# Where the state-space parameters are loaded, when GpSimd starts a round, and five small changes

## The reference, cut to what matters

```python
xn = rmsnorm(x, norm_g);  proj = xn @ w_in          # ten slices: u_a z_a q k v z_b g_a g_b
y_a, h_last = s5_scan(u_a, h0, A, log_dt, B, C, D)  # 64 groups of 16 channels, 64 complex states
y_a = gelu(y_a);  y_a = y_a * sigmoid(y_a @ glu_w + glu_b) * silu(z_a)
o = stick_breaking_attention(q, k_all, v_all, bias) * silu(z_b)   # 8 heads of 128
merged = sigmoid(g_a) * (y_a @ w_branch_a) + sigmoid(g_b) * (o @ w_branch_b)
y = rmsnorm(x + merged @ w_out, norm_f)
```

## Time and profile before

| | |
|---|---|
| median of 3 runs | 3057.72 us (3056.51 to 3058.63) |
| the profiled execution: its time / its span | 3058.2 us / 3056.1 us |
| PE busy | 2973.0 us (97%) |
| DVE / ACT / POOL busy | 1354.0 (44%) / 1017.8 (33%) / 478.9 (16%) |
| mean granted TensorE clock | 0.994 |
| DMA, mean over the span | 108 GB/s |
| one round | about 266 us |

### The profile page before, as it was taken

One profiled execution on the slowest core, in us unless ns is written; L12 is line 12 of the kernel. 1 busy time (PEld: TensorE's weight loads), 2 busy tenths in 40 slices (PEclk: granted clock), 3 DMA queues, 4 the chain that ended last, 5 costly groups with the idle time before them and its releaser, 6 DMA issues.

```text
span 3056.1 us, 48771 instructions
## 1 busy us (share of the span) xinstructions
PE 2973.0 (97%) x19132; PEld 2908.1 (95%) x19132; DVE 1354.0 (44%) x2556; ACT 1017.8 (33%) x1210; POOL 478.9 (16%) x1126
## 2 busy tenths in 40 slices
PE   5999999999999999999999999999999999999997
PEld 5999999999999999999999999999999999999997
DVE  6624443462444346244434524443465444422266
ACT  6135215413521541352154136115422321211142
POOL 6400330050033015003301400330013000000000
PEclk8999999999999999999999999999999999999999
DMA  6231333233223323323322331332438754342283
GB/s 180 79 105 56 87 83 100 72 80 104 63 83 83 98 72 82 105 67 81 84 91 72 86 105 63 91 81 87 138 122 293 247 188 156 94 129 69 79 245 111
DMA packets 425730, 329.29 MB, mean 108 GB/s; under 512 B 64738, under 2 KB 387890, under 8 KB 423474
## 3 DMA queue, kind: packets, MB, share of 16 engines
q1 hardware_dynamic: 425522, 326.34, 35.6%
HBM read 235.72 MB, written 73.73 MB: 101 GB/s over the span
## 4 chain that ended last, share of the span: by engine, by line
PE 78%; POOL 6%; DVE 6%; issue 3%; SPq 3%; ACT 2%; DMA 2%; POOLq 0%; DVEq 0%; ACTq 0%
PE acc L1794 70%; PE side L1759 3%; PE side L1935 2%; DMA work<-work 1%; SPq L501 1%; POOL work L1253 1%; POOL work L1256 1%; POOL work L1254 1%; PE side L1930 1%; POOL work L1259 1%; POOL work L1255 1%; ACT w_high L901 1%; POOL work L1260 1%; DVE work L1528 1%; DMA work<-t_state_seeds 0%
## 5 line engine op out<-in xcount | busy, mean ns | idle before, releaser
L1794 PE MATMUL acc<-x_high,w_high 128*128 128x344 f32 (+2 forms) x5440 | 1221.2, 327 | 16.1 <-ACT w_high L901 3.6
L1794 PE MATMUL acc<-x_low,w_high 128*128 128x344 f32 (+2 forms) x5440 | 1181.0, 320 | 0.0
L1794 PE MATMUL acc<-x_high,w_low 128*128 128x344 f32 (+2 forms) x5440 | 1177.0, 319 | 0.0
L1794 PEld LDWEIGHTS acc<-x_high,w_high 128*128 128x128 f32 x5440 | 908.6, 188 | 37.5 <-issue 17.6
L1794 PEld LDWEIGHTS acc<-x_low,w_high 128*128 128x128 f32 x5440 | 921.8, 189 | 0.0
L1794 PEld LDWEIGHTS acc<-x_high,w_low 128*128 128x128 f32 x5440 | 913.0, 188 | 0.0
L1373 DVE TENSOR_TENSOR w_low<-w_raw,w_high 128x1024 fp32r<-128x1024 f32 x233 | 294.6, 1264 | 612.2 <-ACT w_high L901 609.2
L901 ACT CAST w_high<-w_raw 128x1024 fp32r<-128x1024 f32 x232 | 242.3, 1044 | 940.7 <-PE acc L1794 863.9
L1244 POOL COPY work<-s_tables 128x28 f32 x16 | 3.3, 208 | 1521.1 <-DMA work<-t_state_seeds 1487.7
L1521 DVE TENSOR_TENSOR work<-work,side 128x128 f32<-128x128 f32 x64 | 18.4, 288 | 317.4 <-PE side L1935 317.4
L1759 PE MATMUL side<-work 128*128 128x128 f32 (+5 forms) x704 | 129.4, 312 | 10.0 <-POOL work L1263 10.0
(11 more groups left out here) (305 smaller groups left out, 2435.3 us busy)
## 6 DMA issues: line engine op xcount, KB each, us to landing
w_raw<-in_w_in SPq DMA_DIRECT2D x160, 512.0 KB, 3.9
w_raw<-in_w_out SPq DMA_DIRECT2D x48, 512.0 KB, 3.9
work<-t_sig_ga SPq DMA_DIRECT2D x24, 516.0 KB, 4.2
out<-work SPq DMA_DIRECT2D x18, 512.0 KB
t_qk<-stage SPq DMA_DIRECT2D x16, 516.0 KB, 5.1
work<-t_qk SPq DMA_DIRECT2D x16, 516.0 KB, 4.5
t_sig_gb<-stage SPq DMA_DIRECT2D x16, 516.0 KB, 4.4
t_sig_ga<-stage SPq DMA_DIRECT2D x16, 516.0 KB, 4.3
```

Source lines behind the costliest of these rows:

```text
L1794: ins = mm(acc[s][:, a, 0:n], w[b][:, kk, :], x[:, kx, c0:c0 + n], start=start, stop=stop)
```

## The change

1. `s5_params` of half 0 becomes `load_s5`. For round 0 it is called ahead of the first round; for the others at chunk 19 of the round in front, behind waits for the last scan of attention (`arg_ready`), for `ha_ready` and for `kv_sent`. The small buffers `pw`, `turn` and `u_new` move to the end of the work buffer.
2. GpSimd's half 0 waits for `oz_ready` of the last attention block (step 79) as well as for the parameters.
3. KM of half 0 moves from step 12 to step 11.
4. In the prologue VectorE scales tiles 6 and 7 (between `x_low` of tiles 2 to 5) in place of ScalarE, and ScalarE writes `S_neg` and `S_in` in place of VectorE.
5. The product of keys and query (8 tokens) moves from GpSimd to VectorE, ahead of the sum.
6. TensorE's first column of branch a waits for the seventh GLU gate, its second for the eighth; before, the first waited for the eighth.
7. `new_sums` is cut into pieces at points 21, 22 and 23; the square root and the scaling of the new rows follow at 24 and 25 instead of 22 and 23.

```diff
@@ build
+    c.at = WORK - (12 * HG + 6 * HG + NEW)
     pw = c.take(12 * HG)
@@ sync
+        def load_s5(g0):
+            Bv = [x[0, bass.ds(g0, HG)].rearrange("g n c -> n g c") for x in (B_re, B_im)]
+            sp.dma_start(BcX[0:64], Bv[0]).then_inc(s5_in, 16)
...
+            for f in range(2):
+                sp.dma_start(h12[:, f], t_h[f][...]).then_inc(s5_in, 16)
+        load_s5(0)
@@ s5_params(hf), hf == 0
-                    sp.wait_ge(oz_sent, i * 16 + PRIMED)
-                    sp.wait_ge(kv_sent, i * 80 + PRIMED)
+                    sp.wait_ge(arg_ready, i * 8 + 8 + PRIMED)
+                    sp.wait_ge(ha_ready, i * 2 + 2)
+                    sp.wait_ge(kv_sent, i * 80 + 80 + PRIMED)
+                    load_s5(i * (2 * HG) + 2 * HG)
@@ sync phase_a, after ahead(cn) and send
                 if cn == 0:
+                    sp.wait_ge(oz_sent, i * 16 + PRIMED)
+                    s5_seeds(0)
+                if cn == CHUNKS - 1 and not last:
                     s5_params(0)
-                    s5_seeds(0)
@@ step table
-    ..., KM, ... = ..., (12, 27), ...
+    ..., KM, ... = ..., (11, 27), ...
@@ scalar, prologue
-        act.wait_ge(den_ready, 3)
-        for n in (6, 7):
-            nc.scalar.mul(x_block(n), x_block(n), nrstd[:, NEW + n:NEW + n + 1]).then_inc(x_scaled_a, 1)
+        act.wait_ge(par_mm, 3)
+        nc.scalar.mul(S_neg[0:64]..., acc[0][0:64, 0, :]..., -1.0)
+        nc.scalar.copy(S_in..., acc[0][:, 0, :]...).then_inc(s_seed_ready, 1)
@@ gpsimd
-                if hf == 1:
+                if hf == 0:
+                    pool.wait_ge(oz_ready, 8 * i + PRIMED)
+                else:
                     pool.wait_ge(y_mm, 2 * i + 1)
...
-        for b in range(NEW):
-            pool.wait_ge(pg_k[b % 2], 32 * (b // 2 + 1))
-            pool.wait_ge(q_in[b % 2], 16 * (b // 2 + 1))
-            nc.gpsimd.tensor_tensor(kb, kb, qbc[b % 2]..., ALU.mult).then_inc(kq_done, 1)
@@ vector, prologue
-        for n in range(2, KT):
+        for n in range(2):
+            x_low(2 + 2 * n)
+            x_low(3 + 2 * n)
+            scale(6 + n)
+        for n in range(6, KT):
             x_low(n)
@@ vector, branch a
-                dve.wait_ge(kq_done, n + 1)
+                dve.wait_ge(pg_k[n % 2], 32 * (n // 2 + 1))
+                dve.wait_ge(q_in[n % 2], 16 * (n // 2 + 1))
+                ch(V.tensor_tensor(kb, kb, qbc[n % 2]..., ALU.mult))
@@ vector, last output part
                 if at == 21:
-                    new_sums()
+                    new_added()
+                if at == 22:
+                    new_sums(range(2))
                 if at == 23:
+                    new_sums(range(2, 4))
+                    new_variance()
+                if at == 25:
@@ tensor, branch a
-        pe.wait_ge(glu_n, FT)
         for n in range(KT):
-            if n >= 2:
+            if n < 2:
+                pe.wait_ge(glu_n, FT - 1 + n)
+            else:
                 pe.wait_ge(br_a, n - 1)
```

More of the change, by code:

```diff
@@ L308, in build @@
     pg_in, pg_k, pg_v, q_in = sem("pages_in"), [sem("page_k0"), sem("page_k1")], [sem("page_v0"), sem("page_v1")], [sem("q_in0"), sem("q_in1")]
-    kq_done, zs_part, zs_tr, sarg_ready, sl_ready, sw_ready, sw_tr, swt_ready, spv_mm, ozs_ready = [sem(s) for s in
-        ("kq_done", "zs_part", "zs_tr", "sarg_ready", "slog_ready", "sw_ready", "sw_tr", "swt_ready",
+    zs_part, zs_tr, sarg_ready, sl_ready, sw_ready, sw_tr, swt_ready, spv_mm, ozs_ready = [sem(s) for s in
+        ("zs_part", "zs_tr", "sarg_ready", "slog_ready", "sw_ready", "sw_tr", "swt_ready",
          "spv_mm", "ozs_ready")]
@@ L453, in s5_params @@
                 if hf == 0:
-                    sp.wait_ge(oz_sent, i * 16 + PRIMED)
-                    sp.wait_ge(kv_sent, i * 80 + PRIMED)
+                    sp.wait_ge(arg_ready, i * 8 + 8 + PRIMED)
+                    sp.wait_ge(ha_ready, i * 2 + 2)
+                    sp.wait_ge(kv_sent, i * 80 + 80 + PRIMED)
+                    load_s5(i * (2 * HG) + 2 * HG)
                 else:
                     sp.wait_ge(ha_ready, i * 2 + 1)
-                g0 = i * (2 * HG) + hf * HG
-                Bv = [x[0, bass.ds(g0, HG)].rearrange("g n c -> n g c") for x in (B_re, B_im)]
-                sp.dma_start(BcX[0:64], Bv[0]).then_inc(s5_in, 16)
-                sp.dma_start(BcX[64:128], Bv[1]).then_inc(s5_in, 16)
-                sp.dma_start(BmX[0:64], Bv[1]).then_inc(s5_in, 16)
-                sp.dma_start(BmX[64:128], Bv[0]).then_inc(s5_in, 16)
-                for f in range(2):
-                    sp.dma_start(h12[:, f], t_h[f][:, bass.ds(g0 * NEW, HG * NEW)].rearrange("p (g b) -> p g b", g=HG)).then_inc(s5_in, 16)
+                    load_s5(i * (2 * HG) + HG)
             def s5_seeds(hf):
@@ L866, in _ @@
         nc.scalar.mul(C_neg.rearrange("p (a n) -> p a n", a=2), side[:, :, :], -1.0).then_inc(seed_ready, 1)
+        act.wait_ge(par_mm, 3)
+        nc.scalar.mul(S_neg[0:64].rearrange("p (g b) -> p g b", b=NEW), acc[0][0:64, 0, :].rearrange("p (b g) -> p g b", b=NEW), -1.0)
+        nc.scalar.copy(S_in.rearrange("p (g b) -> p g b", b=NEW), acc[0][:, 0, :].rearrange("p (b g) -> p g b", b=NEW)).then_inc(s_seed_ready, 1)
         for n in range(KT + 3, KT + 5):
@@ L1116, in _ @@
                     nc.scalar.activation(hstd1[:, :], hvar1[:, :], ACT.Sqrt).then_inc(std_ready, 1)
-                if at == 22:
+                if at == 24:
                     act.wait_ge(var_ready, 6)
@@ L1682, in weigh, with new_added @@
             c2(V.tensor_tensor(hs, hs, nf[:, f, :].unsqueeze(1).broadcast_to([P, B2, P]), ALU.mult))
-        def new_sums():
+        def new_added():
             dve.wait_ge(osm_tr, 1)
@@ L1689, in new_sums @@
                                    acc[s][0:NEW, 1:3, :].rearrange("p a (f n) -> p (a f) n", f=4), ALU.add))
-            for q in range(4):
+        def new_sums(quarters):
+            for q in quarters:
                 sq = stage[q % 2][0:NEW, 768:768 + 2 * P].rearrange("p (f n) -> p f n", f=2)
@@ L1695, in new_sums, with new_variance @@
                     c2(V.tensor_reduce(newsum[0:NEW, 2 * q + e:2 * q + e + 1], sq, axis=AX.XY, op=ALU.add))
+        def new_variance():
             n8 = newvar[0:NEW, :]
@@ L1781, in x_transposes @@
             for b in range(4):
-                if k == 0 and 4 * half + b < 6:
+                if k == 0:
                     pe.wait_ge(x_scaled_v, 4 * half + b + 1)
-                elif k == 0:
-                    pe.wait_ge(x_scaled_a, b - 1)
                 last = tr(x_bank(n)[:, b * P:(b + 1) * P], x_block(4 * half + b)[:, k, :], ident[:, :])
```

17 lines of the change are left out of this document (9 added, 8 removed).

## The result

| | before | changed |
|---|---|---|
| median of 3 runs | 3057.72 us | 3031.97 us (3030.60 to 3033.47) |
| profiled execution: its time / its span | 3058.2 / 3056.1 us | 3033.47 / 3031.7 us |
| ratio of times, 95% interval | | 0.9907 (0.9894 to 0.9920) |

The quotient of the two medians is 0.9916 (25.8 us) and lies inside the interval; the ratio in the table is not this quotient and stands for 28 us. The forecast for a median was 3033 with a range of 3027 to 3045. Between the two profiled executions the sum of the terms was 24.6; their spans differ by 24.4. Eight terms that come out within 0.2 in sum need not be right one by one, so the trace is read term by term first.

A forecast was written before the change was run, and what follows sets the result against it. TensorE, busy for 97% of the span, was taken as the bound, with at most 83 us to win. 4.85 + 9.1 + 3.3 + 1.7 + 1.7 + 1.5 + 0.5 + 1.9 = 24.6 off 3058.2 gave 3033.6, median 3033, range 3027 to 3045.

The forecast's parts named there:

- KM one step up (4.85 + 9.1): Rounds: KM at step 11 removes TensorE's waits at YM of half 0 (4.85 us) and KM of half 1 (9.1).
- left-over of 0.13 per round: KM of half 1: wait for GpSimd expected to remain, 0.13 us per round, making 10.0 us into 9.1.
- the prediction's sign against itself: Forecast wrong if GpSimd's half 1 still begins at a landing, or a branch a column waits above 2 us.
- The early start gives TensorE nothing by itself: Rounds: GpSimd's half 0 starts 8.9 us earlier, worth nothing alone to TensorE, but lets KM move a step up.
- Prologue and round 0 (3.3): Start of the kernel to YM of round 0: the chain comes 3.3 us sooner, bounds 1 and 6.
- the 0.7 of the seeds: Round 0: part of GpSimd's first start coming about 2.0 us earlier, 0.7 of it from the state seeds.
- The clock (1.7 + 1.7): Low clock behind standstills: 1.7 us back in round 7, 1.7 in round 0 (bounds 0 and 3.4).
- GLU (1.5): GLU stage: the key product off GpSimd ends TensorE's 1.5 us wait for a low part, bounds 0 and 1.5.
- Branch a (+0.5): Branch a: the earlier door gives 1.2 us, a late low part takes 0.7, leaving 0.5; bounds -2.8 and 1.2.
- the price of the slid queue: Branch a: VectorE's queue slides about 2.3 us once, at column 0, so TensorE stands about 0.7 at column 6.
- Rival C: Branch a: the key product enters the loop feeding it, 27.7 us in standstills and clock, 3062 us in all; chance 0.03.
- Last part (1.9): Last part: cutting point 21's adding into three removes TensorE's 1.9 us standstill, bounds 0.5 and 2.5.

The follow-up runs named there:

- early_only: The kernel before with half 0's parameters loaded early and GpSimd's half 0 started early, KM still at step 12: 3055.86 us, ratio 0.9991.
- km11_only: The kernel before with only KM of half 0 moved from step 12 to step 11: 3039.71 us, ratio 0.9934 to the kernel before.
- no_prologue: The changed kernel with ScalarE scaling tiles 6 and 7 again and VectorE writing the state seeds: 3031.04 us, ratio 0.9906 to the kernel before.
- keys_door: The kernel before with only the key products on VectorE and branch a's door opened by the seventh gate: 3056.42 us, ratio 0.9988.
- keys_twice: The changed kernel with the product of keys and query made twice for each token: 3036.12 us, ratio 0.9922 to the kernel before.
- km12: The changed kernel with KM of half 0 back at step 12: 3051.73 us, ratio 0.9969 to the kernel before.

## Why the prediction was right, step by step

The main mechanism was right, and so were its places. That the sum came within 0.2 us is luck: the rounds and the GLU stage gave 2.8 us more than forecast, the clock of round 7 and branch a 2.6 less.

- **KM one step up (4.85 + 9.1).** Right in place and mechanism: YM's waits of rounds 1 to 6 are gone, GpSimd's half 1 begins behind TensorE's output and stands off by nothing but 0.24 in round 7. The term was too small, 13.95 against 16.3 and, in the kernel with that edit alone, 17.2. Missing was the 0.2 us that each standstill costs over its bracket, which over 13 of them is 2.5, and most of the left-over of 0.13 per round did not come; the waits once a round, 7.5 for 6.5, took 1.0 back. Round 7's half 1 is still released by a DMA, in the one round whose wait was the longest; the prediction's sign against itself came true there, and it cost 0.24.
- **The early start gives TensorE nothing by itself.** Right for the rounds (early_only). But the prediction let step 11 depend on it ("at GpSimd's old pace that is level with `n_ready`"), and km11_only shows that it does not in the rounds: `n_ready` stayed ahead there. What edits 1 and 2 are worth is in round 0, where only the load (edit 1) can act.
- **Prologue and round 0 (3.3).** The sum came out (3.0), the working in part. Right was the place of the zeros, 1.2 of at most 1.28, and that TensorE's head start would be stood off at YM. GpSimd's start gave 1.6 in these two executions where 2.0 were forecast, but none of it is the 0.7 of the seeds: no_prologue puts edit 4 at nothing. The rest is `load_s5(0)` ahead of the first chunk. The prediction had named the chain as what counts and read its last link only (YM behind 1502), not the middle, where rotations that run for 18 us wait for powers that they don't read.
- **The clock (1.7 + 1.7).** Round 0's half came back (1.5), as the windows show (0.66 before, 0.83 now). Round 7's window went (1.54), and one of the same depth came in at 2154 (1.25), so 0.3 of 1.7 was left. The failed step is "Round 7's wait goes, and its 1.7 with it".
- **GLU (1.5).** Right, 1.98 in the changed kernel and in keys_door. The bracket of 1.5 was taken as the upper bound; the stage gained 0.5 more.
- **Branch a (+0.5).** Mis-sized for this execution: -0.7 here, and -1.5 to +1.5 in the five other traces of the same code, +0.1 in the mean of the six. Product (2.28 for 2.3) and door (1.2) were right, the price of the slid queue was 0.7 in the prediction and 0 to 2.7 in six traces. Rival C's loop exists, but keys_twice shows that its price at double the load is 3 to 5 us and not 27.7.
- **Last part (1.9).** 2.05; no row of the wait is left. It had no experiment of its own.

## What to carry over

Follow a wait back until its chain reaches something that waits without need, and move a step there: one number in the table of steps gave 20 of 28 us (by ratios), one wait on the tables instead of the powers a further 4 to 5, and both were found by reading who ends last before a product of TensorE. A gain on an engine that then waits for another chain is no gain (edit 4), and should be priced at nothing until that chain is shown to move too. A term under about 2 us that depends on when transfers land should be read in several executions before it gets a sign.

## What the runs showed of the hardware

- **A standstill's length does not say what clock it costs.** km11_only stood 3.42 us at YM of round 0, and the window behind it is at 1.00:

```profile
120.00:130.00 10.00, 9.56 (x72) 9.08 (x73) 1.95 (x7) 2.04 (x5) 4.37 (x14) 1.00 0.39 105
```

  km12 stood 2.73 at the same product and was granted 0.54 in the same window, mostly the level of 1.2 GHz, which lost 4.6 us of ten:

```profile
120.00:130.00 10.00, 10.00 (x48) 9.12 (x47) 0.19 (x1) 1.46 (x5) 6.00 (x23) 0.54 0.16 35
```

  The same standstill of 2.32 behind ScalarE stands in round 7 of all fourteen traces. A low window is behind it in nine of them, the changed kernel's among these, and none in five, among them the kernel before; its cost up to TensorE's last small product of the rounds was 0.5 to 1.3 us. And a standstill of 3.2 near 94 left a mean clock of 0.72 in 90 to 100 in keys_door, one of 3.27 in km12 left 1.00. This agrees with what the Trainium skill, page "TensorE: Matmul & The Clock Gate", section "What's actually happening", says: the moment of the change of level is not tied to the kernel's own start. By these traces both clock terms needed a range that starts at nothing, and that of round 0 one up to 4.6 us.
- **VectorE beside GpSimd.** GpSimd's product of 128x2048 took 5.05 us and stretched VectorE's instruction beside it from 1.23 to 5.53; VectorE alone makes the product in 2.28. Beside GpSimd's second product a weight split of VectorE took 5.64 (2257.95), beside the six in branch a such splits took up to 2.00; with the products on VectorE they take 1.22 or 1.23. Not everything is stretched: line 1624, which reads TensorE's result, took 1.23 in the middle of a product (2311.01), as without one.
- **The same landing, up to 2.7 us apart.** The parameters of round 0 released GpSimd between 65.48 and 68.18 in four executions with the same order of loads.
